# Two transformer blocks on one core: TensorE's waits taken bank by bank at norms and copies, weight splits moved ahead of copies, local attention's queries turned between the units of the first gate

## The reference

```python
def first_block(x, ...):
    h = rms_norm(x, norm_mix_w)
    z, xbc, dt_raw, q, k, v, f_raw = split(h @ w_in)
    y_ssd = ssd_mixer(xbc, z, dt_raw, ...)       # causal conv of 4 taps, SiLU, Mamba-2 scan
                                                 # in chunks of 128, 16 heads, gated norm
    y_fox = fox_mixer(q, k, v, f_raw, ...)       # q, k normalised per head; causal softmax
                                                 # attention with a forget bias, 16 heads
    x = x + concat(y_ssd, y_fox) @ w_out
    hf = rms_norm(x, norm_ffn_w)
    return x + (silu(gate) * val) @ w_down       # gate, val = causal conv of hf @ w_up

def second_block(x, p, ...):
    h = rms_norm_2(x, mix_norm_g)
    rq, rk, rv, rg, sq, sk, sv, gate_r, gate_s = split(h @ w_in)
    y_r = (silu(rg) * head_group_norm(retention(rq, rk, rv))) @ w_ret_o    # 4 heads of 128
    y_s = sliding_window_gqa(norm(sq), norm(sk), sv, sinks) @ w_swa_o      # 8 heads, 2 kv
    x = x + (sigmoid(gate_r) * y_r + sigmoid(gate_s) * y_s) @ w_out
    x = x + hierarchical_moe(rms_norm_2(x, ffn_norm_g), ...)               # 32 experts, top 2
    return x + sigmoid(rms_norm_2(x, g) @ w_ple_gate) * rms_norm_2(p @ w_ple, ...)
```

## Time and profile before

| | |
|---|---|
| time, median of 3 runs | 1791.22 us (1790.89 to 1798.72) |
| the profiled execution: its own time, its span | 1797.27 us, 1795.1 us |
| mean granted clock of PE | 0.971 |
| PE busy | 1664.7 us, 93%, 7682 matmuls |
| PE's weight loads, beside the matmuls | 1304.8 us, 73% |
| DVE, ACT, POOL busy | 1065.4 us (59%), 868.3 us (48%), 157.2 us (9%) |
| read from HBM | 261.61 MB, 159 GB/s read and written over the span |

### The profile page before, as it was taken

How to read it: one execution, slowest core, us unless ns; L and a number is a source line. 1 busy time by engine, 2 the same in 40 slices (tenths; PEclk the granted TensorE clock), 3 DMA queues, 4 the chain that set the end, 5 groups by cost and what they waited for, 6 DMA issues and landing times.

```text
span 1795.1 us, 24756 instructions
## 1 busy us (share of the span) xinstructions
PE 1664.7 (93%) x7682; PEld 1304.8 (73%) x7682; DVE 1065.4 (59%) x1845; ACT 868.3 (48%) x1561; POOL 157.2 (9%) x170
## 2 busy tenths in 40 slices
PE   5989999898999999999999989999699999999937
PEld 5777788656878888888788877778566767667626
DVE  4747844684345666642423465545677888788663
ACT  4546633574234555522332245433476777677532
POOL 0004200000000000000000010000112212112100
PEclk9999999999999999999999999999889999999969
DMA  5323233210423333333332122223479999999831
GB/s 177 107 83 94 78 115 96 63 57 13 128 77 96 98 95 98 95 98 95 101 98 83 53 88 65 65 80 100 147 242 332 333 341 339 320 346 318 278 141 47
DMA packets 138939, 254.88 MB, mean 142 GB/s; under 512 B 22304, under 2 KB 22560, under 8 KB 138736
## 3 DMA queue, kind: packets, MB, share of 16 engines
q1 hardware_dynamic: 121968, 227.59, 39.5%
q0 software_dynamic: 15088, 21.78, 3.8%
q10 hardware_dynamic: 1808, 4.53, 0.7%
HBM read 261.61 MB, written 24.71 MB: 159 GB/s over the span
## 4 chain that ended last, share of the span: by engine, by line
PE 82%; DVE 9%; ACT 4%; DMA 2%; issue 2%; POOL 1%; ACTq 0%; SPq 0%; DVEq 0%; POOLq 0%
PE ps L325 22%; PE ps L326 22%; PE ps L327 22%; PE ps L937 7%; DMA raw<-in_wexp 2%; PE ps L921 2%; DVE lo L320 2%; PE ps L428 1%; DVE acc L1917 1%; DVE HTl L393 1%; ACT Pb L1806 1%; PE ps L528 1%; PE ps L1582 1%; PE ps L1434 1%; PE ps L1570 1%
## 5 line engine op out<-in xcount | busy, mean ns | idle before, releaser
L320 DVE TENSOR_TENSOR lo<-raw,hi 128x512 fp32r<-128x512 f32 x304 | 208.4, 709 | 319.1 <-ACT hi L310 318.4
L310 ACT ACTIVATE hi<-raw 128x512 fp32r<-128x512 f32 x304 | 184.7, 632 | 389.8 <-PE ps L327 381.8
L325 PE MATMUL ps<-HTh,lo 128*128 128x512 f32 x688 | 273.6, 398 | 20.0 <-DVE HTl L393 6.4
L326 PE MATMUL ps<-HTl,hi 128*128 128x512 f32 x688 | 270.9, 394 | 0.0
L327 PE MATMUL ps<-HTh,hi 128*128 128x512 f32 x688 | 270.6, 393 | 0.0
L1062 ACT ACTIVATE hi<-raw,cst 128x512 fp32r<-128x512 f32 x304 | 207.0, 722 | 88.7 <-PE ps L327 56.0
L1068 DVE SCALAR_TENSOR_TENSOR lo<-raw,cst,hi 128x512 fp32r<-128x512 f32 x304 | 212.4, 749 | 48.5 <-ACT hi L1062 48.3
L325 PE MATMUL ps<-hi,HTl 128*128 128x512 f32 (+1 forms) x416 | 164.2, 395 | 5.1 <-DVE HTl L393 2.8
L325 PEld LDWEIGHTS ps<-HTh,lo 128*128 128x128 f32 x688 | 131.0, 190 | 50.8 <-DVE HTl L393 12.4
L327 PE MATMUL ps<-hi,HTh 128*128 128x512 f32 (+1 forms) x416 | 160.1, 385 | 0.0
L326 PE MATMUL ps<-lo,HTh 128*128 128x512 f32 (+1 forms) x416 | 160.1, 385 | 0.0
(11 more groups left out here) (373 smaller groups left out, 2787.0 us busy)
## 6 DMA issues: line engine op xcount, KB each, us to landing
raw<-in_wstream SPq DMA_DIRECT2D x384, 256.0 KB, 2.7
raw<-in_wexp SPq DMA_DIRECT2D x312, 256.0 KB, 7.1
rawd<-in_wexp SPq DMA_DIRECT2D x39, 1024.0 KB, 8.3
cum<-cum_d POOLq DMA_DIRECT2D x16, 256.0 KB, 3.7
fcb<-fc_d POOLq DMA_DIRECT2D x16, 256.0 KB, 3.5
YG<-ye_d ACTq DMA_DIRECT2D x4, 1024.0 KB, 9.3
X<-in_x SPq DMA_DIRECT2D x4, 512.0 KB, 5.8
xg_d<-xn POOLq DMA_DIRECT2D x4, 512.0 KB, 4.3
```

Source lines behind the costliest of these rows:

```text
L310: act.activation(hi[:, i % RING, :], raw[:, i % RING, :], ACT.Copy).then_inc(hi_ready, 1)
L320: dve.tensor_tensor(lo[:, i % RING, :], raw[:, i % RING, :], hi[:, i % RING, :].bitcast(F32), ALU.subtract).then_inc(lo_ready, 1)
L325: pe.matmul(o, al, bh, start=start, stop=False)
L326: pe.matmul(o, ah, bl, start=False, stop=False)
```

## The change

`pe_tokens` and `pe_features` get an argument `free`: a semaphore and a base, on which the first unit waits in front of each bank. It is used at the norms, at xbc2, at z0, and at q1 to v1; the same waits are written out at retention's scores, skv and the second to fourth gates. Splits are moved ahead of ACT's and DVE's copies at v1, at the last values of out0, at skv and at gr0. z0's small transposes come first, in banks 7 and 6. q0 ends in front of the transposes of Y1. k is turned first. gr0 goes into banks 4 to 7, with the turns of sq behind its fifth unit and those of kd behind its seventh; the norm of sq is made apart from that of sk, with a pow each. The semaphore dec_cp goes; tok_ready counts both copies.

```diff
-        def pe_tokens(pe, u, nk, s, Lh, Ll, k0=0, ready=None, first=True, last=True):
+        def pe_tokens(pe, u, nk, s, Lh, Ll, k0=0, ready=None, first=True, last=True, free=None):
...
                 for t in range(T):
+                    if free is not None and c == 0 and free[1] + t + 1 > 0:
+                        pe.wait_ge(free[0], free[1] + t + 1)
                     mm = mm3(pe, ps[:, 4 * s + t, :], Lh[:, k0 + c, t * P:(t + 1) * P], Ll[:, k0 + c, t * P:(t + 1) * P],
...
         def PE_B2(pe):
-            pe.wait_ge(ht_lo, 20)
-            pe_features(pe, U["rq"], 8, 0, HTh, HTl, ready=(ht_lo, 16))
+            pe_features(pe, U["rq"], 8, 0, HTh, HTl, ready=(ht_lo, 16), free=(ht_lo, 16))
...
-            pe.wait_ge(b2c, 16)
             for h in range(RH):
+                pe.wait_ge(b2c, 13 + h)
...
-            pe.wait_ge(b2c, 20)
             for i in range(4):
                 pe.wait_ge(lo_ready, U["skv"] + i + 1)
                 for t in range(T):
+                    if i == 0:
+                        pe.wait_ge(b2c, 17 + t)
...
+            def gates0(u0, u1):
+                for i in range(u0, u1):
+                    u = U["gr0"] + i
+                    pe.wait_ge(lo_ready, u + 1)
+                    for j in range(4):
+                        mm = mm3(pe, ps[:, 4 + j, :], hi[:, u % RING, j * P:(j + 1) * P], lo[:, u % RING, j * P:(j + 1) * P],
+                                 HTh[:, i, :], HTl[:, i, :], i == 0, i == 7)
+                    mm.then_inc(unit_used, 1)
+            pe.wait_ge(yr_t, RH)
+            gates0(0, 5)
             pe.wait_ge(b2c, 24)
-            pe_features(pe, U["gr0"], 8, 0, HTh, HTl)
             pe.wait_ge(qk_n, 1 + 1)
-            pe.wait_ge(yr_t, RH)
             for c in range(4):
                 for t in range(T):
-                    tr = pe.transpose(ps[:, 4 + c, t * P:(t + 1) * P], sq[:, t, c * P:(c + 1) * P], ident[:, :])
+                    tr = pe.transpose(ps[:, c, t * P:(t + 1) * P], sq[:, t, c * P:(c + 1) * P], ident[:, :])
                 tr.then_inc(s_tr, 1)
+            gates0(5, 7)
...                                               # kd turned into banks 0 and 1
-            pe.wait_ge(b2c, 28)
+            gates0(7, 8)
...
             def gates(u0, u1):
                 for i in range(u0, u1):
-                    if i in (8, 16):
-                        pe.wait_ge(b2c, 28 + i // 2)
                     for j in range(4):
+                        if i % 8 == 0:
+                            pe.wait_ge(b2c, 25 + i // 2 + j)
...
         def ACT_B2(act, w, ch):
-            w.beside(U["skv"] + 4, [copy(sq[:, j, :], ps[:, j, :], "sq", after=((ry_mm, 4),)) for j in range(4)])
+            w.upto(U["skv"] + 4)
+            for j in range(4):
+                copy(sq[:, j, :], ps[:, j, :], "sq", after=((ry_mm, 4),))()
...
-            w.beside(U["gr0"] + 8, [copy(skv[:, j, :], ps[:, j, 0:256], "skv") for j in range(4)])
-            w.upto(U["gr1"] + 7)
+            w.upto(U["gr0"] + 4)
+            for j in range(4):
+                copy(skv[:, j, :], ps[:, j, 0:256], "skv")()
+            w.upto(U["gr1"] + 5)
...                                               # sqT; then splits to gr1 + 7, gr0's copies, gr1 + 8
         def DVE_B2(dve, w, ch):
-            w.upto(U["gr0"] + 4)
...                                               # squares and sums of sq
+            dve.tensor_scalar(sst[:, 1, :, 0:8], sst[:, 0, :, 0:8], 1.0 / HD, EPS, ALU.mult, ALU.add).then_inc(qk_ss, 1)
+            w.upto(U["gr0"] + 4)
...                                               # squares and sums of sk, then the same for 8:10
         def POOL_B2(pool):
-            pool.wait_ge(qk_ss, 1 + 1)
-            pool.tensor_tensor(sst[:, 2, :, :], sst[:, 1, :, :], ...)
+            for i, (h0, n) in enumerate(((0, 8), (8, 2))):
+                pool.wait_ge(qk_ss, 2 + i)
+                pool.tensor_tensor(sst[:, 2, :, h0:h0 + n], sst[:, 1, :, h0:h0 + n], ...)
...
         def _(pe):                                # the first block
-            pe.wait_ge(cvD, 4)
-            pe_features(pe, U["xbc2"], 8, 0, HTh, HTl)
+            pe_features(pe, U["xbc2"], 8, 0, HTh, HTl, free=(cvD, 0))
...
             def turn_x(m):
                 if m >= 4:
                     pe.wait_ge(xs_ready, m - 3)
+                else:
+                    pe.wait_ge(cvD, 9 + m)
+                if m in (0, 8):
+                    pe.wait_ge(xbc_ready, (8, 12)[m // 8])
...
             pe.wait_ge(cvD, 8)
-            stream("z0", 0, 4)
-            pe.wait_ge(xbc_ready, 12)
-            pe.wait_ge(cvD, 12)
...                                               # the decay rows, now into banks 7 and 6
+            stream("z0", 0, 4, free=(tok_ready, -2))
             turn_x(0)
             turn_x(1)
             stream("z0", 4, 5)
...
-            stream("q0", 3, 7)
+            stream("q0", 3, 8)
...                                               # Y1 transposed
-            stream("q0", 7, 8)
             for b in range(1, 6):
-                if b == 1:
-                    pe.wait_ge(mix_lo, 8)
-                else:
-                    pe.wait_ge(qkv_copied, 4 * (b - 1))
-                pe_tokens(pe, U["qqkkvv"[b] + str(b % 2)], 8, (b + 1) % 2, HTh, HTl)
+                pe_tokens(pe, U["qqkkvv"[b] + str(b % 2)], 8, (b + 1) % 2, HTh, HTl,
+                          free=(mix_lo, 4) if b == 1 else (qkv_copied, 4 * (b - 2)))
+            pe.wait_ge(qk_n, 1)
+            pe.wait_ge(qkv_copied, 20)
             for c in range(DC):
-                for i, src in enumerate((q, k)):
+                for i, src in ((1, k), (0, q)):
...
-                        pe.wait_ge(qkv_copied, 24)
+                    elif i == 0:
+                        pe.wait_ge(qkv_copied, 21 + c)
...
         def _(act):
+            w.upto(U["out0"] + 7)
             for t in range(T):
                 copy_qkv(5, t)()
...                                               # qT here, then the split of out0 + 7
             for c in range(DC):
                 if c == DC - 1:
+                    w.upto(U["out0"] + 15)
                     output(c)
...
         def _(dve):
             w.upto(U["z1"])
+            dve.wait_ge(dec_mm, 1)
+            dve.tensor_copy(decB, ps[:, 6, 0:4 * H1]).then_inc(tok_ready, 1)
+            dve.wait_ge(tok_mm, 1)
+            dve.tensor_copy(tok[:, 0:3, :, :].rearrange("p a t h -> p (a t h)"), ps[:, 7, 0:384]).then_inc(tok_ready, 1)
             w.beside(U["z1"] + 4, [conv_x(2, m) for m in range(4)])
...                                               # kT behind w.upto(out0 + 7), MIXl1 as on ACT
```

More of the change, by code:

```diff
@@ L353, in pe_tokens_last, with pe_features @@
                     mm.then_inc(unit_used, 4)
-        def pe_features(pe, u, nk, s, Rh, Rl, ready=None, slot=None):
+        def pe_features(pe, u, nk, s, Rh, Rl, ready=None, slot=None, free=None):
             for c in range(nk):
@@ L362, in pe_features @@
                 for j in range(4):
+                    if free is not None and c == 0:
+                        pe.wait_ge(free[0], free[1] + j + 1)
                     mm = mm3(pe, ps[:, 4 * s + j, :], hi[:, w, j * P:(j + 1) * P], lo[:, w, j * P:(j + 1) * P],
@@ L638, in output @@
                 act.activation(ysh[r, h // 2, :], ps[r, 2, :], ACT.Copy).then_inc(fx_hi, 1)
+            w.upto(U["gr1"] + 7)
             for j in range(4):
-                copy(gr[:, j, :], ps[:, j, :], "gr0", ACT.Sigmoid, after=((ys_n, 1 + T),))()
+                copy(gr[:, j, :], ps[:, 4 + j, :], "gr0", ACT.Sigmoid, after=((ys_n, 1 + T),))()
+            w.upto(U["gr1"] + 8)
             weights(0)
-            w.upto(U["gr1"] + 8)
             for h in range(SH):
@@ L752, in DVE_B2 @@
                                   sst[:, 2, t, 0:8].unsqueeze(2).broadcast_to([P, 8, HD]), ALU.mult)
+            dve.wait_ge(rpow, 1 + 2)
+            for t in range(T):
                 for r in range(2):
@@ L756, in DVE_B2 @@
             ins.then_inc(qk_n, 1)
+            w.upto(U["gr1"] + 3)
             for h in range(RH):
@@ L981, in PE_PLE @@
             pe_norm(pe, 4, xn4, [(x_res, 32), (ye_a, TILES), (ye_b, TILES)])
-            pe.wait_ge(ht_lo, 36)
-            pe_tokens(pe, U["pg0"], 8, 0, HTh, HTl, ready=(ht_lo, 32))
+            pe_tokens(pe, U["pg0"], 8, 0, HTh, HTl, ready=(ht_lo, 32), free=(ht_lo, 32))
             pe_tokens(pe, U["pg1"], 8, 1, HTh, HTl)
@@ L1372, in _ @@
             pe_norm(pe, 0, xn, [])
-            pe.wait_ge(ht_lo, 4)
-            pe_features(pe, U["xbc0"], 8, 0, HTh, HTl, ready=(ht_lo, 0))
+            pe_features(pe, U["xbc0"], 8, 0, HTh, HTl, ready=(ht_lo, 0), free=(ht_lo, 0))
             pe.wait_ge(ht_lo, 8)
@@ L1386, in _, with stream @@
             pe_features(pe, U["xbc1"], 8, 1, HTh, HTl)
-            pe.wait_ge(cvD, 4)
-            pe_features(pe, U["xbc2"], 8, 0, HTh, HTl)
-            def stream(name, c0, c1):
```

(16 more changed lines are left out.)

43 lines of the change are left out of this document (19 added, 24 removed).

## The result

The changed kernel took 1750.47 us (median of 4, 1749.35 to 1753.53) against 1793.18 (median of 4, 1790.89 to 1798.72) beside it: ratio 0.9745, 95% interval 0.9724 to 0.9766. The forecast was 1753.3, a saving of 37.9. The medians lie 42.7 apart, the two profiled executions 46.3 (1797.27 and 1750.96). A second set of executions of the same two programs gave 1750.58 against 1795.38, ratio 0.9755 (0.9729 to 0.9780).

What follows compares the result with a forecast made beforehand. The prediction took TensorE (PE), busy 1664.7 of 1795.1 us, as the bound. Waits of 31.0 plus clock of 6.9 made 37.9 us, taken off the median 1791.22: 1753.3 us, range 1745 to 1773.

Steps and rivals of the forecast that it cites:

- norms 6.0: At three later norms PE starts three HTl pieces earlier, 2.0 us each; nothing won at the first: 6.0 us.
- z0 2.5: At z0's turns a wait of 4.8 us goes, a new one of 2.3 for ACT's xs copy comes: 2.5 us.
- gr0 7.0: Between skv and the first local scores, waits of 2.9 on skv's copies and 4.1 on skT go: 7.0 us.
- gr0's chain: Norm of q and k behind gr0's fifth unit: squares, POOL's pows of 5.7 and 1.4, scaling; ready with margin 3.1 us.
- Clock: Low stretches at xbc2, skv and first local scores return to full clock: 6.9 us of 12.9 in all.
- At the norms 0.8 of idle and the thin transposes stay, at z0 2.3: nothing: Remaining idle at two norms and z0 keeps their low stretches, 1.7 us each and 2.6: no clock gain counted.
- the prediction's upper end: Clock gain across all the low stretches behind PE's waits: 12.9 us back, against a lower end of -1.7.
- the rule of micro-idles: Frequent micro-idles as banks are cycled make the clock oscillate; waits bank by bank could keep low stretches: saving 31.0, not 37.9.
- 1 (no clock back): Waits shrink, but short pauses at each bank keep or move the low stretches: saving 31.0, 1760.2 us; chance 0.20.
- 2 (waits move): ACT and DVE later than reckoned at z0, q and k, gr0: saving 25.6, 1765.6 us; chance 0.13.
- 3 (given back among the experts): Experts' stage ends with its DMA bytes, only the last norm's 2.0 us stays: 1789.2 us; chance 0.05.
- 4 (clock falls in dense stages): Projections and feed-forward part run at low clock; slower from 62 us more, 1800 us at 80; chance 0.05.

Runs made afterwards that it cites:

- the doses: Changed kernel with longer waits put back at norms, in the second also at xbc2; three kernels: 1756.28, 1760.90 and 1764.15 us, one execution each.
- the first two experiments: Waits bank by bank at the four norms alone in the kernel before: 1785.55 us, ratio 0.9939; gr0 put back in the changed kernel: 1763.39 us, ratio 0.9820.

## Why the prediction was right, and where it was off

*Waits.* The sum was 31.0 and measured 30.9, term by term: norms 6.0 (5.5), xbc2 1.9 (2.2), z0 2.5 (2.7, with a new wait of 2.1 for the forecast 2.3), q0 1.6 (1.7), q and k 4.4 (4.1), out0 2.8 (2.8), rg 1.4, skv and sq 2.0, gs0 1.4 (as said), gr0 7.0 (7.1). The first norm's wait on lo stayed, as said. At xbc2 it is 1.8 when the pause at the fourth bank is taken off. gr0's chain held: the two pows took 5.8 and 2.1 us for the forecast 5.7 and 1.4 and ended at 1007.04, and the turn of sq came without a wait at 1013.47. One sum in the prediction is off: 8 x 2.70 + 1.9 + 0.9 is 24.4, not 24.6; 24.51 was measured.

*Clock.* This is the term that was mis-sized: 6.9 were forecast, 12.8 measured. The three places counted came nearly as reckoned: xbc2 1.7 for 1.7, skv and the first local scores 5.0 for 5.2. Wrong was the step "At the norms 0.8 of idle and the thin transposes stay, at z0 2.3: nothing". The norms alone, put into the kernel before, gave the clock back at once, and the doses show what decides: behind the 0.89 us that is left the clock never fell there, behind a wait of 2.1 it fell each time. That is 3.2 us. At z0 the low stretch went as well in the profile after, worth about 2.0 by the starts of the matmuls (the small transposes take 1.1 us instead of 1.9, the turns 1.3 less), where (1-g)L had 2.6. But it came back in three of the eight profiles with the wait of 2.1, so neither nothing nor the whole was the fair count. The heads' 1.5 stood in no term and is chance: their wait of 2.58 never changed, and their stretch was 1.6 us longer in some executions of programs that are alike up to there. That the total comes close to the 12.9 of the prediction's upper end is therefore in part luck.

Had the waits only been broken up into pauses between the banks, the low stretches would have stayed by the rule of micro-idles (Trainium skill, TensorE: Matmul & The Clock Gate, "A second HAM failure mode: psum-queue depth-cycling"). No run here tests that rule: behind the wait of 0.9 at a norm the matmuls start 0.22 to 0.24 us apart from the second on, so that no pauses between the banks arose, and PE ran at 1.00.

*The rest.* 1.7 in the experts' stage, 0.7 at the router and 0.3 before the first product are put down to no part of the change; why they went is not shown. The stage took between 429.7 and 438.8 us in ten profiles in which its code was the same, and 435.7 and 437.0 in two with the old program.

*Off the median.* The saving was worked out on one execution and taken off the median of the runs. The profiled execution before lay near the highest of its runs, the one after near its median, so 46.3 between profiles is 42.7 to 44.8 between medians. That the forecast time came within 2.8 us is luck in part: the saving was 4.8 to 8.4 us too small, but the base of 1791.22 was low as well; with more runs the kernel before had medians of 1793.18, 1795.38 and 1798.06.

*The rivals.* 1 (no clock back) is refuted by the first two experiments. 2 (waits move) is refuted by the waits: besides the one forecast on xs, a single new one of 1.2 us on fst came in the first forgetting heads, where PE at full clock runs into DVE. 3 (given back among the experts): the stage began 42.9 us earlier and was no longer. 4 (clock falls in dense stages): no stretch of the table became longer than by 0.01 us, and PE's busy time fell by 15.7.

Where the prediction said that the same matmuls behind gaps of under 1 us would have to run at 1.2 GHz to refute it, they ran at 2.4.

## What to carry to other kernels

A wait for the fourth of eight pieces costs its own length and often a stretch at a low clock behind it: shortening it from 2.8 to 0.9 us gave 1.9 and 1.6. So when pricing a shortened wait, look not at whether idle time remains but at whether waits as short as what remains are followed by a low clock anywhere in the trace. And judge edits of 2 us by landmarks in the profile, rather than by the total, which here moves by 4 to 9 us with the experts' stage. From the first forgetting scores to ysl identical code repeats to 0.1 us where the clock is the same; in front of z1, at the heads and at the router a stretch can differ by 1 to 3 us, and the granted clock has to be read beside it.

## What was not expected of the hardware

- The low stretches mostly cost about 1.6 us or twice that, and behind the same wait they did not come in every execution (z0's turns: three of eight).
- The very first products ran at 1.00 at once when the wait in front was 1.50 or 0.96 instead of 6.12, although PE had done only transposes until then.
- A low clock can cost nothing where another engine sets the pace, but only up to a point: with 0.91 over their first 20 us the forgetting heads took as long as with 1.00 (three profiles), with 0.83 they took 2.8 us longer (two).
